# Two-pass value product in attention, and the heads' weight strips rounded on GpSimd

## What is computed

```python
q = (rms_norm(c_q, g_q) @ w_uq).reshape(B, S, 16, 96)          # 64 plain + 32 rotated columns
kv = (rms_norm(c_kv, g_kv) @ w_ukv).reshape(B, S, 16, 64 + 64)
k_n, v = kv[..., :64], kv[..., 64:]
for blk in range(S // 128):                                    # causal, blocks of 128 queries
    s = (q_n @ k_n.T + q_r @ k_r.T) * scale                    # masked
    p = softmax(s)
    outs.append(einsum('bhqk,bkhd->bqhd', p, v[:, :k_end]))
o = concatenate(outs).reshape(B, S, 16 * 64)
h = h + o @ w_o
```

## Time and profile before

| what | value |
|---|---|
| time before, median of 3 runs | 1216.26 us (1215.56 to 1216.5) |
| the profiled execution's own time | 1215.19 us |
| its span, first to last instruction | 1213.4 us |
| mean granted TensorE clock | 0.998 |
| busy share: PE, DVE, ACT, POOL | 99%, 50%, 37%, 23% |
| chain that ended last | PE 81% of the span, every other engine 1% or less |

### The profile page before, as it was taken

How to read it: one execution, slowest core, us unless ns; L and a number is a source line. 1 busy time by engine, 2 the same in 40 slices (tenths; PEclk the granted TensorE clock), 3 DMA queues, 4 the chain that set the end, 5 groups by cost and what they waited for, 6 DMA issues and landing times.

```text
span 1213.4 us, 15687 instructions
## 1 busy us (share of the span) xinstructions
PE 1196.4 (99%) x6094; PEld 1011.2 (83%) x6094; DVE 602.4 (50%) x824; ACT 453.8 (37%) x726; POOL 278.7 (23%) x285
## 2 busy tenths in 40 slices
PE   7999999999999999999999999999999999999998
PEld 6778888888888888888879899988888888888887
DVE  6766666454334334344357645657443443433432
ACT  5467777433213222122334245544321221221234
POOL 2334234242002002012212135533210110210211
PEclk9999999999999999999999999999999999999999
DMA  6211112222332323322233434412233233332221
GB/s 188 53 36 29 25 36 94 80 89 85 105 104 90 97 91 104 104 83 91 73 103 105 148 92 97 117 35 92 82 105 104 71 103 104 104 104 81 92 74 71
DMA packets 117498, 107.43 MB, mean 89 GB/s; under 512 B 21334, under 2 KB 115764, under 8 KB 117436
## 3 DMA queue, kind: packets, MB, share of 16 engines
q1 hardware_dynamic: 117404, 106.56, 28.4%
q10 hardware_dynamic: 32, 0.01, 0.0%
HBM read 104.45 MB, written 2.11 MB: 88 GB/s over the span
## 4 chain that ended last, share of the span: by engine, by line
PE 81%; DVE 1%; issue 0%; ACT 0%; POOLq 0%; POOL 0%; DVEq 0%; ACTq 0%
PE ps L1590 25%; PE ps L1592 25%; PE ps L1591 25%; PE ps L2017 1%; PE ps L2019 1%; PE ps L2018 1%; PE ps L2046 1%; PE ps L2048 0%; PE ps L2047 0%; PE ps L1869 0%; PE ps L1871 0%; PE ps L1870 0%; PE ps L2029 0%; PE ps L1939 0%; PE ps L1616 0%
## 5 line engine op out<-in xcount | busy, mean ns | idle before, releaser
L741 ACT CAST whi<-raw 128x2048 fp32r<-128x2048 f32 (+3 forms) x149 | 184.9, 1271 | 265.2 <-PE ps L1592 254.7
L1124 DVE TENSOR_TENSOR wlo<-raw,whi 128x2048 fp32r<-128x2048 f32 (+3 forms) x90 | 197.6, 2198 | 151.3 <-ACT whi L741 151.2
L1590 PE MATMUL ps<-xl,whi 128*128 128x512 f32 (+1 forms) x624 | 245.1, 393 | 0.2 <-issue 0.2
L1591 PE MATMUL ps<-xh,whi 128*128 128x512 f32 (+1 forms) x624 | 243.0, 389 | 0.0
L1592 PE MATMUL ps<-xh,wlo 128*128 128x512 f32 (+1 forms) x624 | 242.9, 389 | 0.0
L1590 PE MATMUL ps<-ul,whi 128*128 128x512 f32 x576 | 224.7, 390 | 0.3 <-DVE wlo L1124 0.3
L1592 PE MATMUL ps<-uh,wlo 128*128 128x512 f32 x576 | 224.2, 389 | 0.0
L1591 PE MATMUL ps<-uh,whi 128*128 128x512 f32 x576 | 224.1, 389 | 0.0
L651 POOL TENSOR_TENSOR ul<-sq,uh 128x512 fp32r<-128x512 f32 x64 | 83.6, 1308 | 521.2 <-ACT uh L973 521.2
L1342 DVE TENSOR_TENSOR h<-ps,h 128x512 f32<-128x512 f32 x78 | 53.6, 689 | 181.5 <-PE ps L1592 178.0
L973 ACT CAST uh<-sq 128x512 fp32r<-128x512 f32 x64 | 39.7, 620 | 266.3 <-DVE sq L1374 266.3
(11 more groups left out here) (269 smaller groups left out, 1676.1 us busy)
## 6 DMA issues: line engine op xcount, KB each, us to landing
raw<-in_mlp_w SPq DMA_DIRECT2D x64, 1024.0 KB, 5.3
raw<-in_mlstm_w_in SPq DMA_DIRECT2D x12, 1024.0 KB, 5.3
raw<-in_mla_w_o SPq DMA_DIRECT2D x4, 1024.0 KB, 4.9
raw<-in_mlstm_w_o SPq DMA_DIRECT2D x4, 1024.0 KB, 5.3
raw<-in_mla_w_in SPq DMA_DIRECT2D x3, 1024.0 KB, 5.5
raw<-in_mla_w_uq SPq DMA_DIRECT2D x16, 192.0 KB, 2.5
x_tok<-in_x SPq DMA_DIRECT2D x4, 512.0 KB, 7.8
mx<-m_rows SPq DMA_DIRECT2D x8, 256.0 KB, 3.6
```

What stands on the lines that cost most here:

```text
L741: last = sc.copy(hi, src)
L1124: last = v.tensor_tensor(lo, src, hi.bitcast(F32), ALU.subtract)
L1590: mm(o, ah, bl, start=first, stop=False)
L1591: mm(o, ah, bh, start=False, stop=False)
```

## The change

Four things are edited.

1. `vh` and `vl` become one tile `vhl` of 256 columns for each 128 positions: high even, low even, low odd, high odd. The stationary block is columns 0 to 127 for the even head and 128 to 255 for the odd head. One pass with `pth` now gives high x high in the head's own 64 partitions and low x high in the other 64; a second pass with `ptl` gives high x low and, in the other partitions, low x low, which was left out before. So each head takes two passes of four matmuls.
2. The two halves of the bank have to be added, head by head: ScalarE copies the other 64 partitions to `o_part` (`o_second(h)`, run in head h+1 behind `pt_high(h+1, 1)`), VectorE adds (`o_add(h)`, behind `q_table` in head h+1). `weigh(h)` waits for `o_add(h-1)`. The zero columns and their two memsets go.
3. `o_scaled(i-1)` works on the sum, and stands now at the end of VectorE's even head, behind `q_low`; `o_high(i-1)` stands at the end of ScalarE's even head, behind the last `exp`.
4. The strips of heads 3 to 15 are rounded on GpSimd (`strip_high`), directly ahead of their `strip_low`, in place of ScalarE's `split`.

```diff
+        vhl = A("vhl", [P, TT, 4 * VD], F32R)
+        o_part = A("o_part", [P, S])
...
+            def strip_high(n, kind):
+
+                pool.wait_ge(raw_full[n % 2], raw_count(n))
+                which, value = strip_over(n - 2, gemm_done, q_mm, k_mm)
+                pool.wait_ge(which, value)
+                for src, hi, _ in split_parts(kind, n % 2):
+                    last = g.tensor_copy(hi, src)
+                last.then_inc(whi_ready, 1)
...
                 if head + 3 < HEADS:
+                    strip_high(N_PAIR + head + 3, "kq" if head % 2 else "q")
                     strip_low(N_PAIR + head + 3, "kq" if head % 2 else "q")
...
+            def o_second(head):
+
+                e = head % 2
+                act.wait_ge(w_mm, head + 1)
+                if head >= 2:
+                    act.wait_ge(o_sum, head - 1)
+                sc.copy(o_part[64 * e:64 * e + 64, :], ps[64 - 64 * e:128 - 64 * e, B_PV, :]).then_inc(o_moved, 1)
...
-                    if i:
-                        o_high(i - 1)
...
-                if head + 3 < HEADS:
-                    split(N_PAIR + head + 3, "q" if not second else "kq")
-                elif head + 3 == HEADS:
+                if head:
+                    o_second(head - 1)
+                if head + 3 == HEADS:
                     split(N_WO)
...
+                if i and not second:
+                    o_high(i - 1)
...
+            def o_add(head):
+
+                i, rows = head // 2, slice(64 * (head % 2), 64 * (head % 2) + 64)
+                dve.wait_ge(o_moved, head + 1)
+                if head % 2 == 0 and i >= 2:
+                    dve.wait_ge(o_lo, i - 1)
+                v.tensor_tensor(o_norm(i)[rows, :], ps[rows, B_PV, :], o_part[rows, :], ALU.add).then_inc(o_sum, 1)
...
-                v.tensor_tensor(o_norm(i), bank(B_PV), r_b[:], ALU.mult).then_inc(o_new, 1)
+                v.tensor_tensor(o_norm(i), o_norm(i), r_b[:], ALU.mult).then_inc(o_new, 1)
...
                 for j in range(TT):
-                    mm(ps[:, B_PV, P * j:S], vh[:, j, cols], pth[e][:, j, P * j:S], start=(e + j == 0), stop=False)
-                pe.wait_ge(v_lo, head // 2 + 1)
-                for j in range(TT):
-                    mm(ps[:, B_PV, P * j:S], vl[:, j, cols], pth[e][:, j, P * j:S], start=False, stop=False)
+                    mm(ps[:, B_PV, P * j:S], vhl[:, j, cols], pth[e][:, j, P * j:S], start=(j == 0), stop=False)
                 pe.wait_ge(t_lo, 4 * head + 4)
                 for j in range(TT):
-                    last = mm(ps[:, B_PV, P * j:S], vh[:, j, cols], ptl[e][:, j, P * j:S], start=False,
-                              stop=(e == 1 and j == TT - 1))
+                    last = mm(ps[:, B_PV, P * j:S], vhl[:, j, cols], ptl[e][:, j, P * j:S], start=False,
+                              stop=(j == TT - 1))
```

More of the change, by code:

```diff
@@ L185, in trunk @@
         ckvl = A("ckvl", [P, 2, S], F32R)
-        vh = A("vh", [P, TT, 3 * VD], F32R)
-        vl = A("vl", [P, TT, 3 * VD], F32R)
+        vhl = A("vhl", [P, TT, 4 * VD], F32R)
+        o_part = A("o_part", [P, S])
         prob = A("prob", [P, P * TT * (TT + 1) // 2])
@@ L217, in v_slot, with v_parts @@
             return v_all[:, i, :].rearrange("p (t e n) -> p t e n", t=TT, e=2)
[L219 to L225, removed]
+        def v_parts(low):
+            quarters = vhl[:, :, :].rearrange("p t (r n) -> p t r n", r=4)
+            return quarters[:, :, 1:3, :] if low else quarters[:, :, 0::3, :]
         def prob_of(b):
@@ L343, in trunk @@
         t_mm, t_hi, t_lo = sem("t_mm"), sem("t_hi"), sem("t_lo")
+        o_moved, o_sum = sem("o_moved"), sem("o_sum")
         w_mm, o_new, o_hi, o_lo = sem("w_mm"), sem("o_new"), sem("o_hi"), sem("o_lo")
@@ L587, in _ @@
             g.tensor_copy(maskr[:], mask_s[:]).then_inc(consts, 1)
-            for t in (vh, vl):
-                g.memset(gap_of(t).bitcast(F32), 0.0)
             def norm_adds(norm, end=False):
@@ L627, in v_low @@
                 pool.wait_ge(v_hi, i + 1)
-                g.tensor_tensor(heads_of(vl), v_slot(i), heads_of(vh).bitcast(F32), ALU.subtract).then_inc(v_lo, 1)
+                g.tensor_tensor(v_parts(True), v_slot(i), v_parts(False).bitcast(F32), ALU.subtract).then_inc(v_lo, 1)
             def o_low(i):
@@ L840, in v_high @@
                     act.wait_ge(w_mm, 2 * i)
-                sc.copy(heads_of(vh), v_slot(i)).then_inc(v_hi, 1)
+                sc.copy(v_parts(False), v_slot(i)).then_inc(v_hi, 1)
+            def o_second(head):
[4 more added lines that the diff above has]
+                sc.copy(o_part[64 * e:64 * e + 64, :], ps[64 - 64 * e:128 - 64 * e, B_PV, :]).then_inc(o_moved, 1)
             def o_high(i):
@@ L924, in _ @@
                 attention(head)
+            o_second(HEADS - 1)
             o_high(PAIRS - 1)
@@ L1287, in row_scales @@
                 low(rinv2[:, 8:16], rinv[:], rinv2[:, 0:8]).then_inc(r_inv, 1)
+            def o_add(head):
[4 more added lines that the diff above has]
+                v.tensor_tensor(o_norm(i)[rows, :], ps[rows, B_PV, :], o_part[rows, :], ALU.add).then_inc(o_sum, 1)
             def o_scaled(i):
-                dve.wait_ge(w_mm, 2 * i + 2)
+                dve.wait_ge(o_sum, 2 * i + 2)
                 dve.wait_ge(r_ready, i + 1)
-                if i >= 2:
-                    dve.wait_ge(o_lo, i - 1)
-                v.tensor_tensor(o_norm(i), bank(B_PV), r_b[:], ALU.mult).then_inc(o_new, 1)
+                v.tensor_tensor(o_norm(i), o_norm(i), r_b[:], ALU.mult).then_inc(o_new, 1)
             for e in range(2):
@@ L1310, in attention @@
                     row_scales(i)
-                elif i:
-                    o_scaled(i - 1)
                 if second and nxt:
@@ L1319, in attention @@
                     q_table(head + 2)
+                if head:
+                    o_add(head - 1)
                 if nxt:
@@ L1330, in attention @@
                     q_low(head + 2)
+                if i and not second:
+                    o_scaled(i - 1)
             for head in range(HEADS):
                 attention(head)
+            o_add(HEADS - 1)
             o_scaled(PAIRS - 1)
@@ L1746, in weigh @@
                 e = head % 2
-                cols = slice(VD * e, VD * e + P)
+                cols = slice(P * e, P * e + P)
                 pe.wait_ge(t_hi, 4 * head + 4)
-                pe.wait_ge(v_hi, head // 2 + 1)
-                if e == 0 and head:
-                    pe.wait_ge(o_new, head // 2)
+                pe.wait_ge(v_lo, head // 2 + 1)
+                if head:
+                    pe.wait_ge(o_sum, head)
                 for j in range(TT):
-                    mm(ps[:, B_PV, P * j:S], vh[:, j, cols], pth[e][:, j, P * j:S], start=(e + j == 0), stop=False)
-                pe.wait_ge(v_lo, head // 2 + 1)
-                for j in range(TT):
-                    mm(ps[:, B_PV, P * j:S], vl[:, j, cols], pth[e][:, j, P * j:S], start=False, stop=False)
+                    mm(ps[:, B_PV, P * j:S], vhl[:, j, cols], pth[e][:, j, P * j:S], start=(j == 0), stop=False)
                 pe.wait_ge(t_lo, 4 * head + 4)
                 for j in range(TT):
-                    last = mm(ps[:, B_PV, P * j:S], vh[:, j, cols], ptl[e][:, j, P * j:S], start=False,
-                              stop=(e == 1 and j == TT - 1))
+                    last = mm(ps[:, B_PV, P * j:S], vhl[:, j, cols], ptl[e][:, j, P * j:S], start=False,
+                              stop=(j == TT - 1))
                 last.then_inc(w_mm, 1)
```

## The result

The changed kernel takes 1246.2 us (median of 5 runs, 1244.84 to 1247.71), the kernel before in the same comparison 1215.78: ratio 1.0251, 95% interval 1.024 to 1.0263. It is 30.4 us slower. The forecast was 1235, the range ended at 1246.0; the direction is right, the size is not.

A forecast was written before the change was run, and what follows sets the result against it. TensorE, busy 99%, was taken as the bound. From 1215.19 us, -10.2 + 27.0 + 0.5 + 0.5 = +17.8 gave 1233.0, 1234.1 for the median, 1235 with something for the clock; range 1228 to 1246.

The forecast's parts named there:

- the clock: Six idle stretches of TensorE could halve its clock: nothing to 12.6 us, about 1 taken.
- the first rival: The clock falls at most of TensorE's six stalls, adding 5 to 12.6 us: 1239 to 1247, chance 0.25.
- The stall: TensorE waits 4.5 us for a q strip held on GpSimd behind `o_low`, heads 2 to 12, six times: 27.0 us.
- the hand-overs: Between engines in the chain from `q_low` to the strip: 0.1 us each, strip to matmul 0.15.
- The casts: GpSimd's three casts of a q strip, between `o_low` and the subtraction: 0.98 us.
- The removed pass: One value-product pass fewer on TensorE in each of 16 heads, 0.64 us each: 10.2 us gained.
- The added halves: Copy and addition delay the fourth score group by nothing to 0.15 us a head, 14 heads: 0.5 us taken.
- made `weigh` wait: Nearly 3 us to spare before `weigh`; a rival had it wait for the addition, some tenths a head, inside 0.02.
- The end of attention: Behind the last head TensorE waits about 1.1 us, about 0.6 comes back in head 14: net 0.5 us lost.
- Head 14's wait: TensorE's wait of 0.9 us for VectorE in head 14 shrinks, about 0.6 us back.
- That no stall would remain: Rival: the scaling chain is ready before TensorE leaves the value product, 1207 us, chance 0.05.
- The smaller stall of 2 to 4 us: Rival: GpSimd or VectorE is quicker on SBUF operands, so TensorE's stall is shorter: 1219 to 1229, chance 0.06.

The follow-up runs named there:

- e2: The changed kernel with 18 matmuls on data nobody reads ahead of the strip's wait at the start of heads 3, 5, ... 13: 1234.35 us, ratio 1.0153.
- e3: The changed kernel with the strips' rounding back on ScalarE in its old place, GpSimd still subtracting behind `o_low`: 1234.86 us, ratio 1.0155.
- e1: The changed kernel with GpSimd's `o_low` of the pair before moved behind the rounding and subtraction of the q strip: 1209.34 us, ratio 0.9946.
- e9: e7 with the first pass of the value product done twice in every head: 1216.56 us, ratio 1.0006.
- e7: e1 with VectorE's addition of the halves moved behind `row_max` of the next head's second block: 1208.23 us, ratio 0.9937.
- e4: The changed kernel with rounding and the largest piece of the q strip's subtraction ahead of `o_low`, two small pieces behind: 1226.11 us, ratio 1.0084.

## Why the prediction was wrong

**The step that failed is the clock.** The prediction put it so: "Nothing to 6 x 2.1 = 12.6 us; I take about 1, half of one fall, because before these stalls the engine is fully busy, unlike at the end of the kernel." Being fully busy before protected nothing: at waits of 4.0 us the clock fell six times of six in the profiled execution. What it cost is 1246.2 - 1234.35 = 11.9 us by e2, 2.0 a fall (2.2 by the profiled executions), so the size (2.1 from the first transposes) was right and the count was wrong. It was the first rival, "the clock falls at most stalls", priced 1239 to 1247 with a chance of 0.25. The Trainium skill's warning about idle gaps (TensorE: Matmul & The Clock Gate, Why this matters for your kernels) is borne out by this trace, 0.50 behind each stall, and deserved more weight. The range ended at 1246.0 although this rival alone was priced to 1247.

What stood against that rival can be settled too: "the records show 1.00 through the start's idle gap". It was a misreading. The first clock record in the trace of the kernel before begins only at 11.36 us, about where its slow transposes end, and the view shows 1.00 for a stretch without a record. In e3 the first record begins at 13.62 us, and ahead of it matmuls of 512 columns start 0.42 us apart under a clock shown as 1.00 (timeline and window of e3):

```profile
12.24 0.63 PE L1688 MATMUL ps<-xl,whi 128*128 128x512 f32 x1
12.66 0.63 PE L1689 MATMUL ps<-xh,whi 128*128 128x512 f32 x1
...
12.00:13.00 1.00, 1.00 (x4) 0.70 (x3) 1.00 (x3) 0.14 (x1) 0.74 (x1) 1.00 1.04 298
```

That is the pace of the half clock, as behind the stalls. So the start was no evidence against the rival. Whether the clock fell in its idle gap or had been low from the beginning, no record shows.

**The stall: right, a little too long.** Predicted 4.5 us six times, measured 4.18: 6 x 4.18 = 25.1 against 27.0. By experiment, e2 less e1, 25.0. The chain came out link by link. What was too high were the hand-overs, 0.1 us each, where `o_scaled` starts 0.60 behind `q_low`'s start, 0.08 before that ends, and `o_high` 0.04 behind `o_scaled`'s end; from strip to matmul it was 0.05 and not 0.15. The casts were forecast at 0.98 and took 0.85, with 0.09 until the subtraction. It happened in the six heads named, and at no odd head's strip.

**The removed pass: 10.2 predicted, 8.3 found** (e9 less e7; 8.8 by the profiled executions). The 0.64 us are right for each head where TensorE sets the pace. The step "16 x 0.64" took for granted that it does in the last heads too, although showed a wait of 0.9 us in head 14.

**The added halves: 0.5 predicted for the score group, more found.** The bound (0 to 0.15 us a head) was too low for even heads: 0.32 us by pitch, six times, 1.9 us. The mechanism is the predicted one, with sizes read too favourably. The exponential's second record ends 0.87 us behind the start of the third score group in e1 (120.08 to 120.95), where it was 0.14 in the kernel before: the delay was 0.73 and not 0.5 to 0.7. The score group starts 0.05 behind that record, which leaves 0.48 of the 0.53 of slack. That gives 0.25 us, and the group's first matmul, coming out of a pause, holds the next one up by some 0.06 more. In odd heads the pitch shows no such loss. No copy or addition made `weigh` wait, as predicted.

**The end of attention: about right.** 1.1 us of wait forecast behind the last head (its own terms, 1.5 - 0.48, give 1.0), 0.8 found. Head 14's wait shrank from 0.9 to 0.4 in the changed kernel, but only to 0.6 in e1, where no stall stands ahead of it; 0.6 back had been forecast, 0.3 came.

**The sum**, by differences between runs: e1 less before -6.5 (pass, halves and tail together, forecast -9.2), stall +25.0 (forecast +27.0), clock +11.9 (forecast +1): +30.4, where +18.8 was forecast. The first two terms miss by 2.7 and 2.0 in opposite ways and nearly cancel, which is luck; all but 0.7 us of the error of the whole is the clock.

**The other rivals.** That no stall would remain did not happen: its condition was a chain shorter by 4.5 us. It is what e1 makes, and then the time is 1209, near the 1207 given. The smaller stall of 2 to 4 us did not happen either. It was priced at 1219 to 1229 (by the prediction's own terms 4 us give 1231) with no fall of the clock in it; e4 shows 1226 for waits of 2.15 us and e3 1234.9 for 3.1, both with falls.

**Left open.** Why equal stalls of 3.1 or 2.15 us let the clock fall at some places and not at others was not settled: the stalls of a run differ in when they come, and no run here varied that alone. The split of e3's and e4's time between stall and clock is worked out, not measured: 1209.3 + 6 x 3.3 = 1229 and 1209.3 + 6 x 2.3 = 1223, which leaves 5.8 us for four falls and 3.0 for two, 1.5 each. The falls are counted in one execution and the times are medians; e3's profiled execution, at 1235.88, would give 1.7.

## What to carry to other kernels

When work is moved to the end of an engine's list for the sake of one engine, look at what other engines' in-order lists hold behind it: here a strip that had nothing to do with the scaling waited behind `o_low`, and its reader was the bound. Price a stall of the matrix engine twice, by its length and by the half clock behind it; 4.2 us of standing cost 6.2 here. Where a wait can't be shortened, matmuls that nobody reads, ahead of it, are worth more than idleness (11.9 us here), and where two engines' lists are balanced to 0.5 us, an addition of 0.7 us has a place where it is free (e7, up to head 12) and one where it isn't (e1).

## What was not expected of the hardware

- In the profiled executions the clock fell at 6 of 6 waits of 4.0 us, 4 of 6 of 3.1 us, 2 of 6 of 2.15 us and 0 of 6 of 1.2 us (the last with 12 matmuls ahead of it).
- It can fall after work has resumed: e3's stall ends at 152.15 and the clock goes to 0.50 between 153 and 154, with TensorE fully busy. A trace that shows full speed at the first matmul behind a stall doesn't prove that the stall was free.
- It stays low for long: in the changed kernel 6.8 us at each of the six falls, so that 4.8 to 6.0 us of work has its matmuls of 512 columns start 0.43 us apart in place of 0.23. At both falls of e4 and three of e3's four it was 3.4 us.
- A granted clock shown as 1.00 ahead of the trace's first clock record says nothing: in e3 it stands over matmuls at the pace of the half clock.
- GpSimd's one-input casts are half as dear as its subtraction of the same pieces: 0.85 against 1.55 us for a q strip.
